# Sums of squares over a head's features: two fp32r products of an exact high and low part, taken later, instead of one full-precision product

## The reference

```python
def rms_norm(h, gain):
    h32 = h.astype(jnp.float32)
    h32 = h32 * lax.rsqrt(jnp.mean(h32 * h32, axis=-1, keepdims=True) + EPS)
    return (h32 * gain.astype(jnp.float32)).astype(h.dtype)

# diff_attention (layer 0)
q = rms_norm(q.reshape(B, S, H, 2, hd), q_gain) * (hd ** -0.5)     # hd = 64: two halves of a head
k = rms_norm(k.reshape(B, S, H, 2, hd), k_gain)
...
o = rms_norm(o, subln_gain) * (1.0 - lambda_init)                  # over all 128 features
# hgrn2 (layer 1), a gated linear recurrence
o = rms_norm(o, out_gain.reshape(H, dv)) * jax.nn.silu(g)
```

## Time and profile before

| what | value |
|---|---|
| median of 3 runs | 2408.46 us (2407.95 to 2410.26) |
| profiled execution, first to last instruction | 2407.3 us |
| chain that ended last | PE 92%, DVE 3%, ACT 2%, DMA 1%, issue 1% |
| ACT, DVE busy | 860.6 us (36%), 1273.2 us (53%) |
| attention's stretch | about 408 to 650 us |
| hgrn's stretch | about 1416 to 1674 us |

### The profile page before, as it was taken

How to read it: one execution, slowest core, us unless ns; L and a number is a source line. 1 busy time by engine, 2 the same in 40 slices (tenths; PEclk the granted TensorE clock), 3 DMA queues, 4 the chain that set the end, 5 groups by cost and what they waited for, 6 DMA issues and landing times.

```text
span 2407.3 us, 30397 instructions
## 1 busy us (share of the span) xinstructions
PE 2373.9 (99%) x11034; PEld 1906.8 (79%) x11034; DVE 1273.2 (53%) x1953; ACT 860.6 (36%) x1320; POOL 202.0 (8%) x337
## 2 busy tenths in 40 slices
PE   7999999999999999999999999999999999999998
PEld 5888888677788888888888888888888888867766
DVE  6886334455678873343333355555533333469554
ACT  4222223566543222242222243344422222344443
POOL 1212000000001110000000013331000000120200
PEclk9999999999999999999999999999999999999999
DMA  8899332321259973223333321212233333242211
GB/s 279 277 287 294 111 96 72 98 62 53 70 168 288 289 230 108 86 79 96 96 99 108 90 79 54 62 53 79 86 97 96 96 111 96 69 97 62 62 53 53
DMA packets 420385, 285.27 MB, mean 119 GB/s; under 512 B 22690, under 2 KB 397788, under 8 KB 420304
## 3 DMA queue, kind: packets, MB, share of 16 engines
q1 hardware_dynamic: 397888, 207.64, 29.8%
q0 software_dynamic: 20896, 73.80, 9.3%
q10 hardware_dynamic: 1520, 2.77, 0.3%
HBM read 281.85 MB, written 6.72 MB: 120 GB/s over the span
## 4 chain that ended last, share of the span: by engine, by line
PE 92%; DVE 3%; ACT 2%; DMA 1%; issue 1%; SPq 1%; POOL 0%; ACTq 0%; DVEq 0%; POOLq 0%
PE bank L686 13%; PE bank L688 13%; PE bank L687 13%; PE bank L863 7%; PE bank L861 7%; PE bank L862 7%; PE bank L1530 4%; PE bank L1532 4%; PE bank L1531 4%; PE bank L1557 2%; PE bank L721 2%; PE bank L723 2%; PE bank L722 2%; PE bank L1179 1%; PE bank L1152 1%; PE bank L701 1%
## 5 line engine op out<-in xcount | busy, mean ns | idle before, releaser
L642 DVE TENSOR_TENSOR w_lo<-raw,w_hi 128x1024 fp32r<-128x1024 f32 (+1 forms) x331 | 434.0, 1311 | 423.9 <-ACT w_hi L623 418.4
L623 ACT ACTIVATE w_hi<-raw 128x1024 fp32r<-128x1024 f32 (+1 forms) x331 | 369.7, 1117 | 478.0 <-PE bank L688 243.2
L686 PE MATMUL bank<-h_hi,w_hi 128*128 128x512 f32 x1344 | 523.4, 389 | 1.6 <-DVE w_lo L642 1.6
L687 PE MATMUL bank<-h_lo,w_hi 128*128 128x512 f32 x1344 | 523.3, 389 | 0.0
L688 PE MATMUL bank<-h_hi,w_lo 128*128 128x512 f32 x1344 | 523.2, 389 | 0.0
L686 PEld LDWEIGHTS bank<-h_hi,w_hi 128*128 128x128 f32 x1344 | 252.4, 188 | 54.5 <-DVE w_lo L642 2.4
L687 PEld LDWEIGHTS bank<-h_lo,w_hi 128*128 128x128 f32 x1344 | 252.4, 188 | 52.4
L688 PEld LDWEIGHTS bank<-h_hi,w_lo 128*128 128x128 f32 x1344 | 252.4, 188 | 52.3
L861 PE MATMUL bank<-g_hi,w_hi 128*128 128x512 f32 x704 | 274.5, 390 | 0.0
L863 PE MATMUL bank<-g_hi,w_lo 128*128 128x512 f32 x704 | 274.1, 389 | 0.0
L862 PE MATMUL bank<-g_lo,w_hi 128*128 128x512 f32 x704 | 274.1, 389 | 0.0
(11 more groups left out here) (420 smaller groups left out, 3021.7 us busy)
## 6 DMA issues: line engine op xcount, KB each, us to landing
raw<-in_ffn_w_in SPq DMA_DIRECT2D x176, 512.0 KB, 3.9
ada<-in_ada_w POOLq DMA_DIRECT2D x128, 512.0 KB, 5.0
raw<-in_ffn_w_down SPq DMA_DIRECT2D x64, 704.0 KB, 4.6
raw<-in_hgrn_w_in SPq DMA_DIRECT2D x32, 512.0 KB, 4.0
raw<-in_attn_w_qkv SPq DMA_DIRECT2D x24, 512.0 KB, 3.8
raw<-in_w_in SPq DMA_DIRECT2D x22, 512.0 KB, 3.8
ada_first<-in_ada_w SPq DMA_DIRECT2D x16, 512.0 KB, 10.7
bias_scratch<-bias_lines POOLq DMA_DIRECT2D x14, 320.0 KB, 9.0
```

The source lines that it names most:

```text
L623: line(nc.scalar.activation(w_place(n, 0, k * P)[0], raw[:, n % 4, 0:k * P], ACT.Copy), hi_ready)
L642: line(nc.vector.tensor_tensor(lo, raw[:, n % 4, 0:k * P], hi.bitcast(F32), ALU.subtract), lo_ready)
L686: nc.tensor.matmul(out_ap, wh, xh, start=(k == 0), stop=False)
L687: nc.tensor.matmul(out_ap, wh, xl, start=False, stop=False)
```

## The change

Each sum of squares but one (that of attention's last head) is made of two fp32r products with the same matrix of ones in fp32r: one with the squares' high part, one with the rest. The high part is one more copy on ACT (`squares_hi`), which waits for ACT's own squaring, and the low part one more subtraction on DVE (`squares_lo`). ACT squares the bank first and copies it second. PE waits for the low part. The product stands later in PE's list: in attention behind the row step instead of ahead of it, in hgrn behind the scores and the turned values of i = 1 instead of at i = 0; the steps that use it (`head_scale`, `scaled`) move with it. The new tiles lie on memory that other tiles use at other times. The core of the diff:

```diff
+        def column_sums(bank, weights, hi, lo):
+
+            nc.tensor.matmul(bank[:, :], weights[:, :], hi[:, :], start=True, stop=False)
+            return nc.tensor.matmul(bank[:, :], weights[:, :], lo[:, :], start=False, stop=True)
+
+        def squares_hi(act, line, hi, squares, squared, made):
+
+            act.wait_ge(squared, line.value(squared))
+            line(nc.scalar.activation(hi[:, :], squares, ACT.Copy), made)
+
+        def squares_lo(dve, line, hi, lo, squares, made):
+
+            line(nc.vector.tensor_tensor(lo[:, :], squares, hi[:, :].bitcast(F32), ALU.subtract), made)
+
         H_TILES = [(h_hi[:, k, :], h_lo[:, k, :]) for k in range(KD)]
...
-            line(nc.scalar.activation(osb, B[6][:, :], ACT.Copy))
-            line(nc.scalar.activation(osq, B[6][:, :], ACT.Square), o_sq)
+            line(nc.scalar.activation(osq, B[6][:, :], ACT.Square))
+            line(nc.scalar.activation(osb, B[6][:, :], ACT.Copy), o_sq)
+            squares_hi(act, line, osq_hi, osq, o_sq, o_hi)
...
-                nc.tensor.matmul(B[7][:, :], ones[:, :], osq1[:, :], start=True, stop=True).then_inc(o_ss, 1)
+                if h == HEADS - 1:
+                    nc.tensor.matmul(B[7][:, :], ones[:, :], osq1[:, :], start=True, stop=True).then_inc(o_ss, 1)
+                    return
+                pe.wait_ge(sums_const, 2)
+                pe.wait_ge(o_lo, h + 1)
+                column_sums(B[7], ones_a, osq_hi, osq_lo).then_inc(o_ss, 1)
 
             def aux(b):
-                pe.wait_ge(headsq, b + 1)
                 if b:
                     pe.wait_ge(headrs, b)
                 if b % 3 < 2:
-                    nc.tensor.matmul(B[2][:, :], halves[:, :], sq[:, :], start=True, stop=True).then_inc(headss, 1)
+                    pe.wait_ge(sums_const, 1)
+                    pe.wait_ge(headlo, 2 * (b // 3) + b % 3 + 1)
+                    column_sums(B[2], halves_a, sq_hi, sq_lo).then_inc(headss, 1)
                 else:
+                    pe.wait_ge(headsq, b + 1)
                     for c_ in range(TT):
                         s = slice(c_ * P, (c_ + 1) * P)
                         last = nc.tensor.transpose(B[2][:, s], avT[:, s], ident[:, :])
@@ -1379,10 +1418,10 @@
                         product_part(pe, n0 + b, B[b % 2], half)
...
-                    if half == 0 and b:
-                        aux(b - 1)
                 if b is not None and st is not None:
                     step(st)
+                if b and half == 0:
+                    aux(b - 1)
             u0 = TT * (HEADS - 1)
...
-                    line(nc.scalar.activation((aq, ak)[b % 3][:, h % 2, :], B[b % 2][:, :], ACT.Copy))
-                    line(nc.scalar.activation(sq[:, :], B[b % 2][:, :], ACT.Square), headsq)
+                    line(nc.scalar.activation(sq[:, :], B[b % 2][:, :], ACT.Square))
+                    squares_hi(act, line, sq_hi, sq[:, :], act_own, headhi)
+                    line(nc.scalar.activation((aq, ak)[b % 3][:, h % 2, :], B[b % 2][:, :], ACT.Copy), headsq)
...
+            def outputs_lo(h):
+                if h < HEADS - 1:
+                    dve.wait_ge(o_hi, h + 1)
+                    squares_lo(dve, line, osq_hi, osq_lo, osq1[:, :], o_lo)
             step = rows_dve(dve, line, 0, HEADS, 2,
-                            ((7, lambda h: head_out_dve(dve, line, h, o1[:, h % 2, :], subg_c, ors1[:, :],
+                            ((4, outputs_lo), (7, lambda h: head_out_dve(dve, line, h, o1[:, h % 2, :], subg_c, ors1[:, :],
...
                 if b and half == 0:
+                    if (b - 1) % 3 < 2:
+                        dve.wait_ge(headhi, 2 * ((b - 1) // 3) + (b - 1) % 3 + 1)
+                        squares_lo(dve, line, sq_hi, sq_lo, sq[:, :], headlo)
                     split_lo(dve, line, n0 + b + 1)
...
-                nc.tensor.matmul(B[7][:, :], ones[:, :], sq[:, :], start=True, stop=True).then_inc(o_ss, 1)
+                pe.wait_ge(o_lo, HEADS - 1 + h + 1)
+                pe.wait_ge(sums_const, 3)
+                column_sums(B[7], ones_h, sq_hi, sq_lo).then_inc(o_ss, 1)
 
             def core(h, i):
                 if i == 0:
-                    if h:
-                        sums(h - 1)
+                    pass
                 elif i == 1:
                     pe.wait_ge(f_done, h + 1)
                     pe.wait_ge(q_copied, h + 1)
                     score(h, h * nlev)
                     values(h)
+                    if h:
+                        sums(h - 1)
                 elif i < 9:
                     v = i - 2
                     if v == 0:
...
-                if s == CORE * (HEADS + 1):
+                if s == CORE * (HEADS + 1) + 1:
                     sums(HEADS - 1)
...
-                line(a.activation(ho[:, :], B[6][:, :], ACT.Copy))
-                line(a.activation(sq[:, :], B[6][:, :], ACT.Square), o_sq)
+                line(a.activation(sq[:, :], B[6][:, :], ACT.Square))
+                line(a.activation(ho[:, :], B[6][:, :], ACT.Copy), o_sq)
+                squares_hi(act, line, sq_hi, sq[:, :], o_sq, o_hi)
...
-                if i == 1 and h:
-                    head_scale(h - 1)
-                if s == CORE * (HEADS + 1) + 1:
+                if s == CORE * (HEADS + 1) + 2:
                     nc.scalar.preload_act_table_set("natural_log_exp_and_others")
...
                     value_turned(h)
+                    if h:
+                        head_scale(h - 1)
...
+            def outputs_lo(h):
+                dve.wait_ge(o_hi, HEADS - 1 + h + 1)
+                squares_lo(dve, line, sq_hi, sq_lo, sq[:, :], o_lo)
...
-                    if i == 3 and h:
-                        scaled(h - 1)
                     if kind == "g" and j:
                         low(j - 1)
                     if s == CORE * (HEADS + 1) + 3:
                         scaled(HEADS - 1)
+                if s == CORE * (HEADS + 1) + 1:
+                    outputs_lo(HEADS - 1)
                 if i == 1:
+                    if h:
+                        outputs_lo(h - 1)
                     diagonal(h)
                 elif i is not None and 2 <= i < 9:
                     level(h, i - 2)
+                    if i == 4 and h:
+                        scaled(h - 1)
                 elif i == 10:
                     states(h)
             gated(HEADS - 1)
```

More of the change, by code:

```diff
@@ L156, in program @@
         ada = sb("ada", [P, 4, D])
-        ada_sum = sb("ada_sum", [P, D])
+        ph = ExitStack()
+        ada_sum = sb("ada_sum", [P, D], F32, ph)
+        ph.close()
+        sq_hi = sb("sq_hi", [P, T], F32R)
+        sq_lo = sb("sq_lo", [P, T], F32R)
         ident = sb("ident", [P, P])
@@ L171, in program @@
         lnt = sb("lnt", [P, T])
-        tmp = sb("tmp", [P, 4, T])
+        ph = ExitStack()
+        tmp = sb("tmp", [P, 4, T], F32, ph)
+        ph.close()
+        sb("tmp_begin", [P, 2, T])
+        osq_hi = sb("osq_hi", [P, T], F32R)
+        osq_lo = sb("osq_lo", [P, T], F32R)
         eight = sb("eight", [P, 3, 8])
@@ L210, in program @@
         ors1 = sb("ors1", [P, T], F32, ph)
+        ones_a = sb("ones_a", [P, P], F32R, ph)
+        halves_a = sb("halves_a", [P, P], F32R, ph)
         ph.close()
@@ L227, in program @@
         yh_lo = sb("yh_lo", [P, KD, T], F32R, ph)
+        ones_h = sb("ones_h", [P, P], F32R, ph)
         ph.close()
@@ L316, in program @@
         headss = sem("headss")
+        headhi = sem("headhi")
+        headlo = sem("headlo")
+        o_hi = sem("o_hi")
+        o_lo = sem("o_lo")
+        sums_const = sem("sums_const")
         headrs = sem("headrs")
@@ L1421, in attention_act @@
             n0 = FIRST["QKV"]
+            line(nc.scalar.activation(halves_a[:, :], halves[:, :], ACT.Copy), sums_const)
+            line(nc.scalar.activation(ones_a[:, :], ones[:, :], ACT.Copy), sums_const)
             def aux(b):
@@ L1637, in hgrn_act @@
             n0 = FIRST["HIN"]
+            line(a.activation(ones_h[:, :], ones[:, :], ACT.Copy), sums_const)
             def gates(b, j):
```

## The result

The changed kernel takes 2421.32 us in the median of four runs (2418.84 to 2423.1), the kernel before 2408.64 in four (2407.95 to 2410.26). The ratio is 1.0054, 95% interval 1.0042 to 1.0066: 12.7 us, or 0.5%, slower. The direction was forecast, and the two stages in which it happens, but the loss is larger than the 8.0 of the forecast. The span of the profiled execution grew by 14.2 us (2407.3 to 2421.5).

A forecast was written before the change was run, and what follows sets the result against it. PE, busy 99% of the span, was taken to bound the kernel. Span 2407.3 + 7.0 (hgrn) + 1 (attention) = 2415.3 us, plus 1.2 to the median: 2416.5 forecast, 0.3% slower; 8-in-10 range 2410.5 to 2421.

The forecast's parts named there:

- hgrn, seven heads: Hgrn heads 1 to 7: PE waits 1.30 for the low part behind `w_lo`; each head loses 0.77, together 5.4 us.
- hgrn, last head: Hgrn's last head: no scores or values between, so PE arrives early and the sum ends at +5.13, not 3.49; costs 1.6.
- attention, first two groups: Attention's first two groups: no or few steps to be delayed, so they give back 0.5 us.
- attention, six heads: Attention's repeating heads: waits outweigh the saved 3 x 0.40, each head 0.3 longer, six heads +1.8 us.
- attention, the rest: Attention's tail: the output sum there gives back 0.4 us.
- The price of a sum: Sums on PE: 0.91 in hgrn, 0.86 in attention; two fp32r products take 0.46, saving 0.45 and 0.40.
- the delay is passed on whole: Hgrn, behind PE's wait: ACT and DVE mostly wait for PE's scores, so each head's 0.77 us loss is kept.
- a rival of its own: PE's granted clock falls to 1.2 GHz: 4.2 us per episode, one or two giving 2421 to 2425; chance 0.04.
- the two turned-weights waits: Attention, next two steps after later maxima: PE waits 0.3 and 0.15 us for turned weights.
- The saving: Rival: PE's waits vanish and all or most of the 12.8 us saved shows, 2396 to 2402; chance 0.08.
- Cancelling: Rival: hgrn loses 7, attention's waits are not carried on and it gains 3 or more, 2408 to 2412.5; chance 0.14.
- an attention bound by ACT and DVE: Rival: the loop through DVE and ACT delays every attention head by 1 to 1.5, giving 2421 to 2426; chance 0.08.

The follow-up runs named there:

- both orders mended: Changed kernel with hgrn's low part of the squares ahead of `w_lo` and scaling in its old place, attention as in the kernel before: 2404.56 us, ratio 0.9985.
- all keys early: Changed kernel with hgrn's low part ahead of `w_lo`, scaling in its old place, and all eight attention key sums ahead of the step: 2411.59 us, ratio 1.0011.
- attention alone: Changed kernel with hgrn's three lists as in the kernel before, attention as changed: 2411.61 us, ratio 1.0018.

## Why the prediction was right in kind and too small in size

| term | forecast | measured |
|---|---|---|
| hgrn, seven heads | +5.4 (0.77 each) | +8.0 (1.02, then 1.16) |
| hgrn, last head | +1.6 | +1.8, and 1.7 for the clock |
| attention, first two groups | -0.5 | +0.5 |
| attention, six heads | +1.8 | +1.5 |
| attention, the rest | -0.4 | +0.6 |
| sum | +8.0 | +14.2 in the profile, +12.7 in the medians |

(Of attention's first line, 0.4 that the records of before show too early is taken off its first group and added to its second.)

The median lies 0.3 us above the range of the forecast (2410.5 to 2421). The forecast's mechanism in hgrn held; what failed are terms of its sum, the seven heads of hgrn above all, and a clock term that it did not add.

**What bounds the kernel: right.** PE's list and PE's waits decide; no wait of ACT or DVE alone cost time.

**The price of a sum: 0.07 too low where PE waits.** I took two fp32r matmuls at 0.23 each. Out of a wait the second starts 0.30 to 0.31 behind the first, and the pair is 0.53. Over the 17 sums that PE waited for this is 1.2 us. Where hgrn's PE did not wait, with both orders mended, a head gained 0.44, as forecast.

**Hgrn, heads 1 to 7: mechanism right, term mis-sized.** Chain 5.15 (5.11 forecast), wait 1.33 (1.30). With the pair's 0.53 the quarter of i = 2 is 0.87 late in the first head, as its second weight block shows (1463.16 - 1456.80 in place of 1458.18 - 1452.69 = 5.49). Two terms are missing from the 0.77. First, "the delay is passed on whole" left out `scaled`, which stands on DVE ahead of `w_lo` at i = 4 rather than at i = 3. It costs some 0.15 in each of the seven, the first included, most of it at the level of i = 6, and the run with the scaling in its old place took it back (its first head is 28.89 long where the changed kernel's is 29.04). I had named this step as moved and given it no price. Second, in heads 2 to 7 PE starts the pair 0.26 behind the end of the low part, not 0.10 as in the first head (0.11 forecast), so the chain is 5.30 there. That it is the same with the scaling in its old place shows that it is a cost of its own; in these heads PE's list has one more wait in front of the pair, and whether that is the cause was not tested. 7 x 0.87 + 7 x 0.15 + 6 x 0.15 = 8.0, against 5.4: the largest miss.

**Hgrn, last head: +1.6 was nearly right, and the clock came on top.** Behind the last output hgrn is 3.5 longer, of which 1.7 is the clock; with the scaling in its old place, where the clock stayed, it was 1.9. I held the clock as a rival of its own (0.04), priced at 4.2 for an episode; one came, behind the 2.1 us wait that I had forecast, at 1.7. It belonged into the forecast as an addition, not beside it as an alternative, and for attention's first wait too, where it came in six of seven executions. The rule of the Trainium skill ("TensorE: Matmul & The Clock Gate", section "A second HAM failure mode: psum-queue depth-cycling"), by which frequent short idle times between groups of matmuls make the clock swing, is not borne out by hgrn's waits, once in some 29 us: 1.00 over 1416 to 1650, with seven waits for the low part in it.

**Attention, the settled head: right in size, partly by luck.** Waits of 0.98 and 0.22, +0.3 forecast, +0.29 measured, by a query wait smaller than the forecast 1.2 and a saving that is smaller too; the two turned-weights waits that I had carried on do not show in each head.

**Attention, the ends: wrong.** I gave them gains of 0.9 (0.5 and 0.4) because there are few or no steps that could be delayed; they lost 1.1. The first query sum waits 1.9 (0.95 before), since PE has nothing to do between the two: its first blocks are already made. The end loses 0.6, and shows waits of 0.72 for the last head's scores and 1.33 for turned weights, where before there was one of 0.66. With the last key sum ahead of the step the 0.72 is gone and the end is as long as before, so the late key sum is its cause; the sum's own wait costs as much there.

**The rivals.** The saving does not win here. In hgrn it does with two instructions of DVE exchanged: the point I named (the low part's end before 1456.4) is what this experiment meets, 1455.55 there; but no version came near the 2396 to 2402 that I had given this rival. Cancelling and an attention bound by ACT and DVE did not come.

## What to carry to other kernels

If work is split between engines, the new link has to stand in each engine's list by when it is needed: one instruction of 0.69 us behind one of 1.23, which itself waits for another engine, cost 14 us over eight heads, with all that followed from it (+11.6 against -2.4), and exchanging them on an engine that stood idle gave it all back. A saving of 0.3 to 0.4 us is only worth taking where the consumer would have to come later than the added chain anyway (hgrn's sums behind scores; attention's keys behind the step) and not where it stands directly before the result (attention's queries). Measure stages by a mark that the change doesn't move, and look at the granted clock of a stretch before explaining a difference of one or two microseconds in it: two such differences of this case (attention's +2.6 against +3.4, and 35.8 against 34.2 at its end) were the clock.

## What was not expected of the hardware

- After a single wait of PE the granted clock can fall for a few microseconds, at a cost of 1.7 us each time (0.83 over 10 us). It came behind eight of the ten waits of 1.9 to 2.1 us in the two stages: in attention's first head in six of seven executions, in hgrn's last in two of three. It came once behind a wait of 1.33 (with the query sums as before), and not behind one of 1.78 (with all keys early), nor behind hgrn's seven waits of up to 1.3. The same program can have it in one execution or place and not in the next.
- An fp32r matmul that comes out of a wait, or behind small fp32 products, starts 0.30 to 0.31 us ahead of the next one; directly behind others of its kind it is 0.23, with new operands too (the second sum with attention alone: 427.42, 427.65, 427.88). So a pair takes 0.53 in the one case and 0.46 in the other. The copy into fp32r (0.63) and the subtraction (0.69) cost what their twins had shown.
